# Eight unread matrix products around the routing step of a two-layer hybrid encoder with experts

## The reference

```
g_sel  = argmax(t @ w_rg + b_rg)                     # one of 4 groups
top_p, top_i = top_k(softmax(e_logits of that group), 2)
weights = sum(one_hot(expert_id, 32) * combine)      # 2 of 32 experts per token
for each expert e:  out += (silu(t @ w_gate[e]) * (t @ w_up[e]) * weights[:, e]) @ w_down[e]
```

## Time and profile before

| | us |
|---|---|
| median of 3 runs | 1184.43 |
| lowest, highest | 1184.11, 1186.07 |
| the profiled execution's own time | 1185.0 |
| its span in the trace | 1183.3 |
| TensorE busy | 923.9 (78%) |
| TensorE weight loads | 587.3 (50%) |
| VectorE busy | 354.0 (30%) |
| ScalarE busy | 202.8 (17%) |
| moved from memory | 436.17 MB, 369 GB/s over the span |

### The profile page before, as it was taken

How to read it: one execution, slowest core, us unless ns; L and a number is a source line. 1 busy time by engine, 2 the same in 40 slices (tenths; PEclk the granted TensorE clock), 3 DMA queues, 4 the chain that set the end, 5 groups by cost and what they waited for, 6 DMA issues and landing times.

```text
span 1183.3 us, 26463 instructions
## 1 busy us (share of the span) xinstructions
PE 923.9 (78%) x11004; PEld 587.3 (50%) x11004; DVE 354.0 (30%) x1165; ACT 202.8 (17%) x600; POOL 8.1 (1%) x24
## 2 busy tenths in 40 slices
PE   7999889667678786986699988996666666765954
PEld 6877745333344443553388777453333333433532
DVE  4666343111112232231166645321111111111213
ACT  2275211000001010110124652110000000000001
POOL 2000000000000000000000000000000000000000
PEclk9999989887889998998899999898888888888977
DMA  9853489999999999999996326899999999999995
GB/s 340 319 223 143 151 337 428 429 429 430 429 428 428 429 429 428 412 427 431 405 399 257 124 99 252 353 429 428 430 431 427 431 430 428 431 429 428 428 427 208
DMA packets 50633, 436.17 MB, mean 369 GB/s; under 512 B 9408, under 2 KB 13760, under 8 KB 24640
## 3 DMA queue, kind: packets, MB, share of 16 engines
q1 hardware_dynamic: 50496, 434.26, 88.0%
HBM read 433.20 MB, written 1.05 MB: 367 GB/s over the span
## 4 chain that ended last, share of the span: by engine, by line
PE 46%; DMA 39%; DVE 4%; issue 4%; SPq 2%; DVEq 2%; ACT 1%; ACTq 0%
DMA ring<-in_w_up 38%; PE ps L623 13%; PE ps L711 8%; PE ps L639 5%; PE ps L855 5%; PE ps L648 3%; PE ps L591 3%; PE ps L727 2%; PE ps L611 2%; SPq L462 1%; PE ps L716 1%; DMA ring<-in_w_in 1%; SPq L464 1%; PE ps L824 1%; PE ps L774 1%
## 5 line engine op out<-in xcount | busy, mean ns | idle before, releaser
L623 PE MATMUL ps<-ring,xg 128*32 128x256 f32 x4352 | 314.2, 452 | 173.9 <-DMA ring<-in_w_up 168.6
L623 PEld LDWEIGHTS ps<-ring,xg 128*32 128x32 f32 x4352 | 170.0, 129 | 301.4 <-issue 239.9
L1204 DVE SCALAR_TENSOR_TENSOR th<-th,ps 128x128 f32<-128x128 f32 x72 | 20.7, 287 | 588.1 <-ACT th L977 588.1
L639 PE MATMUL ps<-ring,actT 128*32 128x256 f32 x2304 | 139.2, 382 | 14.1 <-issue 13.2
L977 ACT ACTIVATE th<-ps 128x128 f32<-128x128 f32 x72 | 20.0, 277 | 510.2 <-PE ps L623 474.2
L639 PEld LDWEIGHTS ps<-ring,actT 128*32 128x32 f32 x2304 | 69.0, 109 | 75.3 <-DVE actT L1208 22.6
L591 PE MATMUL ps<-xh,Pb 128*32 128x256 f32 x1152 | 79.5, 394 | 23.4 <-issue 19.4
L711 PE MATMUL ps<-hT,ring 128*128 128x256 f32 x416 | 93.5, 382 | 1.0 <-ACT hT L1014 0.8
L711 PEld LDWEIGHTS ps<-hT,ring 128*128 128x128 f32 x416 | 77.8, 190 | 15.0 <-issue 4.4
L648 PE MATMUL ps<-ysb,PwT 32*128 32x256 f32 x992 | 71.6, 403 | 0.0
L981 ACT ACTIVATE ysb<-ps 128x256 f32<-128x256 f32 x64 | 24.5, 383 | 223.9 <-PE ps L639 223.9
(11 more groups left out here) (259 smaller groups left out, 681.5 us busy)
## 6 DMA issues: line engine op xcount, KB each, us to landing
ring<-in_w_down SPq DMA_DIRECT2D x62, 2048.0 KB, 40.4
ring<-in_w_gate SPq DMA_DIRECT2D x60, 2048.0 KB, 45.2
ring<-in_w_up SPq DMA_DIRECT2D x60, 2048.0 KB, 46.9
ring<-in_w_in SPq DMA_DIRECT2D x6, 2048.0 KB, 15.5
ring<-in_w_out SPq DMA_DIRECT2D x4, 2048.0 KB, 18.6
ring<-in_w_gate SPq DMA_DIRECT2D x8, 1024.0 KB, 29.3
ring<-in_w_up SPq DMA_DIRECT2D x8, 1024.0 KB, 31.3
ring<-in_w_in SPq DMA_DIRECT2D x6, 1024.0 KB, 16.0
```

The costliest lines, as they stand in the source:

```text
L623: last = mm(b_gate[j * SLOTS:(j + 1) * SLOTS, 0:2 * GQ], tokens[:, k, :], ring[:, low:high + 1:high - low, o:o + GQ], start=(k == 0), stop ...
L639: last = mm(b_y[j * SLOTS:(j + 1) * SLOTS, 0:DQ], actT[:, c * SLOTS:(c + 1) * SLOTS], ring[:, slot, o:o + DQ], start=(c == 0), stop=(c == ...
```

## The change

Two stretches of products that nobody reads are added to TensorE's program, in each of the two layers. The new step `busy.0` stands in `ORDER` between `seed` and `wt`; it issues five products of the identity with 256 columns of x into the bank of `fT.1` (bank 4), which has been read by then. Three more such products, into `b_gate` (bank 5), are issued right behind the first gather of a layer. None of the eight has a wait of its own. `busy` is a TensorE step only and claims no bank, so all banks stay as they are, and TensorE's `done` count grows by one more per layer.

```diff
-    xc2.2 sa.0 sa.1 xc2.3 sa.2 fT.0 sd fT.1 fT.2 fT.3 rs2 lg seed wt cnt xn2 rank ov route
+    xc2.2 sa.0 sa.1 xc2.3 sa.2 fT.0 sd fT.1 fT.2 fT.3 rs2 lg seed busy.0 wt cnt xn2 rank ov route
...
-         "sS", "yn", "oS", "cn", "outA", "outB", "fT", "lg", "seed", "cnt", "rank", "ov"}
+         "sS", "yn", "oS", "cn", "outA", "outB", "fT", "lg", "seed", "cnt", "rank", "ov", "busy"}
...
+BUSY = (5, 3)
...
+    if step[0] == "busy":
+        return []
     return [step]
...
+                    elif kind == "busy":
+
+                        for j in range(BUSY[s[1]]):
+                            last = mm(ps[BANK["fT", 1]][:, j % 2 * SEQ:(j % 2 + 1) * SEQ], ident[:, :], x[:, j % 2, 0:SEQ], start=True, stop=True)
...
                 gather(M, Pb[0])
+                for j in range(BUSY[1]):
+                    mm(b_gate[:, 0:SEQ], ident[:, :], x[:, j % 2, 0:SEQ], start=True, stop=True)
                 pe.wait_ge(done["dve"], nth(li, "dve", ("ov",)))
```

## The result

The changed kernel takes 1190.42 us (median of 6 runs, 1188.87 to 1195.49) against 1185.10 (median of 6) for the kernel before, measured beside it: a ratio of 1.0048, 95% interval 1.0033 to 1.0063. It is about 5 us slower, where 1182.7 us and no measurable difference had been forecast. The profiled execution has a span of 1189.0 us, against 1183.3.

The account below looks back on a forecast made before the run. Weight transfers were taken to pace the kernel, except where the ring is full. Layer 1 gave 1.5 us (0.2 count delay deducted), layer 0 nothing; taken as 1.7 for the median: 1184.43 - 1.7 = 1182.7 us, range 1180.9 to 1185.0.

Parts of the forecast that it names:

- The sum: Whole kernel: 1185.0 - 1.5 = 1183.5 us for the profiled execution; 1184.43 - 1.7 = 1182.7 us for the median.
- the delay of the count: Five products behind the seeding make the counting product late; charged 0.2 us, between 0.1 and 0.4.
- the transfers pace everything: Layer 1 from the restart to 1163 us: weight transfers set the pace, so the 1.5 us reach the end.
- Layer 1's restart: First hidden product of layer 1 at full clock: w_down issued 1.5 us earlier; bounds 0.5 and 2.35.
- Layer 0's restart: First w_down of layer 0: SP's parameter loads decide when it is issued, so the gain is 0.
- the bound of -0.5: Layer 0's w_down: bound on the gain of 0 if TensorE becomes late.
- The three behind the gather: Take 1.3 to 1.4 us in 1.47 idle, cost nothing; at half clock 2.6 to 2.8, sticking out 1.1 to 1.3.
- The weight loads: Added products: loads overlap with matmuls, so matmul rows alone set the price; five products cost 2.2 to 2.3 us.
- the rival rule: Added products: loads overlap only across differing row groups; count 2 us late, gain used up, 1184.5 or more; chance 0.02.
- the clock falls all the same: Rival: added products run at half speed before the hidden product; 1.2 us in layer 1, total 1186.2; chance 0.08.

Follow-up runs that it names:

- 1: The kernel before with 16 one-column products (64 instructions) added at the end of TensorE's main program; 1194.74 us, ratio 1.0078.
- run 3: The changed kernel with its eight products one column wide, same instructions at the same places; 1194.83 us, ratio 1.0080.
- run 12: The changed kernel itself measured once more, beside run 11; 1193.07 us, ratio 1.0061 to the kernel before.
- 8: The changed kernel with 32 one-column products at the end, extra blocks moved by 192 instructions in all; 1184.49 us, ratio 0.9993.
- run 4: The kernel before with 32 one-column products (128 instructions) added at the end of TensorE's main program; 1195.56 us, ratio 1.0077.
- run 2: The changed kernel with 48 one-column products at the end, extra blocks moved by 256 instructions in all; 1184.24 us, ratio 0.9988.
- run 11: The changed kernel with 48 one-column products inside layer 1's experts, ahead of the 16th's hidden product; 1183.45 us, ratio 0.9982.
- Run 6: The kernel of run 2 measured again; 1183.78 us, ratio 0.9981 to the kernel before.
- run 10: The kernel before with only the three products behind the first gather, and 58 one-column products at the end; 1187.01 us, ratio 1.0020.
- run 7: The kernel before with only the five products behind the seeding, and 54 one-column products at the end; 1185.31 us, ratio 0.9999.

## Why the prediction was wrong

**The sum lacked a term.** Its steps priced what the eight products do where they stand: the delay of the count, the clock in layer 1, nothing in layer 0 beyond the restart. That they are also 64 more instructions ahead of blocks that are reached by a branch it put at nothing, without a reason. That term is the result: 5.3 us slower instead of 1.7 faster. All runs whose extra blocks were moved by 64 (the change twice, 1 and 3) have a stop of 3.0 to 3.5 us between the 11th and 12th row of the second pass's gather; moved by 256 or not at all, none has; moved by 128 or 192, the second pass waits some 6.5 us ahead of its first product instead. The same section of the Trainium skill ("Runtime: NRT & Kernel Launch", "Instruction fetch mechanics") has the rule: instructions come in blocks of 16 KiB, 256 of them, one after the other, and a taken branch to a target outside what is held has to wait for its block. The packets and the period of 256 agree with it. So does the time of the packets, which the trace holds too. In the stretch from 362.19 to 365.52 us of the changed kernel, the stop, the DMA queues show one packet of instructions:

```profile
q8 instruction: 1, 0.02, 1.8%
```

It begins at 363.2 and takes 0.97 us, and TensorE goes on 1.3 us behind its end; in the stops of 1, 3 and 12 it is 1.3 to 1.4 us. In the waits ahead of a pass TensorE goes on some 3 us behind the end of such a packet (2.9 to 3.1 in the kernel before, the changed one, and 8), and the 11.56 us of run 4 hold two of them. That the border falls behind the 11th row was not worked out from addresses, only found.

**From 3.3 us of stop to 6.3 of loss.** Relative to layer 0's w_down, TensorE reaches the second pass's down product at 209.9 us in the changed kernel and at 204.8 in run 2: 5.1 us later, mostly the stop and a hidden product begun at half clock behind it (4.71 us). A spell of half clock near 415 adds 1.5, a longer wait ahead of a later pass (7.60 us against 6.98) 0.6, and a longer spell of half clock behind that wait, which run 2 has too, 1.4. So the down product of layer 0's last extra pass starts at 326.2 against 317.4 (490.21 and 480.83 less 164.06 and 163.44), 8.8 us later, and so does the w_down that SP could not issue while the ring was full (333.5 against 324.7). At the end of the experts 6.0 us of it are left; what took up the rest was not traced. How much is lost differs between executions of the same kernel: in run 12 it was 9.2 us against run 11. The sentence on what comes behind the restart ("the transfers pace everything") was made for layer 1 and held for it; of layer 0 I looked only at the restart, and had put its experts down as paced by transfers throughout.

**Layer 1's restart: right.** 1.5 us were forecast, w_down 6.5 us after the count; it was 6.36 to 6.37 us in all six profiled executions with both groups of products (the first one, 2, 6, 8, 11 and 12), 1.8 less than before. In these six the first hidden product took 3.66 us in both layers, twelve of twelve. Run 6 puts the whole gain at 2.2 us (0.9981), the forecast for the median at 1.7.

**Layer 0's restart: right.** SP's parameter loads decide: w_down follows the last of them within 0.05 us in 13 of the 14 profiled executions. In run 3, where the clock was low during the seeding and again from the gather to the hidden product, it came 1.6 us behind (163.98 against 162.41), so TensorE can become the later of the two, as the bound of -0.5 allowed for.

**The delay of the count: right in size only where the clock is up** (0.1 us in layer 1: 0.26 us behind `sel` instead of 0.15). With the clock low during the seeding it was 1.7 us.

**The three behind the gather: right.** Their six rows took 1.56 us at full clock, a little over the 1.3 to 1.4 forecast, and the hidden product followed at once, 4.37 us after the count (4.43 before); at half clock they took 2.69 us, as bounded.

**The weight loads: right.** Ten rows with their loads took 2.32 us, against the 2.2 to 2.3 that the matmul rows alone had given. The price of the rival rule was worked out in two ways that don't agree: a count 2 us late, as under the rivals, would have turned the sum of 1.5 into a loss of some 0.5 us, not a gain of 0.5.

**Readings that were wrong without moving the sum.** The slices at 99 and 143 GB/s lie inside the mixers (680 to 710 us and 89 to 118 us), not between mixers and experts; the full rate in layer 0 begins with the seventh slice, not the sixth; and layer 0's hidden product could get only 2.6 us faster (6.24 less 3.66), not 3.3.

**The rivals.** None had the mechanism. The one on the slow side ("the clock falls all the same") showed only in run 10, with the three products alone: the hidden product of layer 1 was 1.0 us late, as priced (1.2), which is far from 5.

## What to carry to other kernels

A change that adds instructions to an engine with far branches moves every block behind it, and this can outweigh what the instructions do. Before an effect of a few microseconds is laid to the change, compare the idle times "issue" inside the branched blocks with those of the kernel before, and run the change once more with its code filled up to 256 instructions, and the old kernel with as many added at a place where they do nothing. To hold the clock up to the work that needs it, count on filling every gap before it: the three products behind the last gap alone did not do it (run 10), and the five before it alone did it in one layer of two (run 7).

## What was not expected of the hardware

TensorE can stop for 3.0 to 3.5 us between the two matmul rows of one product, and it stood idle for some 6 to 8 us at two of the far branches of layer 0's experts (6.46 and 6.21 in the kernel before, 6.82 and 7.60 in the changed one), once 11.56, but under 1.2 us at others. The granted clock falls at places that differ from one execution to the next and from layer to layer, also in the seeding. The same program spreads over 6.6 us (1188.87 to 1195.49); in most of the runs the slower executions have the lower mean clock, but that the clock makes the whole spread is not shown.
